# Two index-query units in one opening, the bias table in another visit, one weight load held back

## The chip, the cores and the metric

The kernel runs on 1 core of a Trainium2 chip. Its time is the device time of one execution in microseconds (us). Three runs of the kernel before gave 461.08, 461.11 and 461.12 us, the median is 461.11 us. TensorE is called PE here, VectorE DVE, ScalarE ACT, GpSimd POOL, and SyncE, which only issues transfers, SP.

## What is computed

One layer with two token mixers side by side: a gated linear recurrence (HGRN2), and a sparse attention in which a small indexer picks the keys. The input is 512 tokens of 1024 channels; one wide projection feeds everything. What the change touches is the indexer (projections `qi`, `ki`, `wi`) and the relative-position bias of the attention.

```python
proj = jnp.einsum('bld,dn->bln', x, w_in) + b_in
qa, fa, ia, za, qb, kb, vb, zb, qi, ki, wi, ga, gb = jnp.split(proj, cuts, axis=-1)
...
dots = jnp.einsum('bthd,bsd->bths', qi, kif) * (IDX_DIM ** -0.5)
score = jnp.einsum('bth,bths->bts', wb * (IDX_HEADS ** -0.5), jax.nn.relu(dots))
score = jnp.where(causal[None], score, -jnp.inf)
_, idx = lax.top_k(score, topk)
...
logits = jnp.einsum('bthd,btkhd->bhtk', qh, ks) * (HEAD_DIM_B ** -0.5)
bias = rel_bias[t5_bucket(qpos[None, :, None] - idx)]
p = jax.nn.softmax(logits + bias, axis=-1)
...
merged = jax.nn.sigmoid(ga) * ua + jax.nn.sigmoid(gb) * ub
return layer_norm(ALPHA * x + jnp.einsum('bld,de->ble', merged, w_out), ln_g, ln_b)
```

## The kernel before

The order of all work is written out by hand: each engine has a program of its own, and semaphores tie them together. The projection is cut into 31 units of 256 output columns (`UNITS`; unit 0 is `kiwi`, the index keys and index weights, with 72 columns), and four units of the output projection follow. Each engine's program walks over quarters q of a unit: unit u has the quarters 4u to 4u+3, of 12 matmuls each. What an engine does beside the units at a quarter stands in its `side(q)`. Such an insertion into PE's row of unit matmuls is called a visit here: the index dots (`dots`, from quarter 12 on), the scores and their transposes, the tree of the recurrence (`tree`).

Every product is made in three matmuls, as both operands are split into a rounded high part and a low part: hi x hi, hi x lo, lo x hi (`split_product`, L511 to L513). The contraction of 1024 runs over eight tiles k of 128. So a unit needs, per tile, a piece of the weights (512 KB per half of a unit, transfer on SP's queue into `w_raw`, which has two places, u % 2), ACT's rounding to `w_hi` (L825), and the subtraction that gives `w_lo`. POOL does that subtraction for most units (L1637), DVE for units 0 and 1 and for late ones (L1458). The input's tiles are treated alike: `x_in` (L467), `x_hi` by ACT (L843), `x_lo` by DVE (L1166).

The opening is special, since the input itself is only arriving. `opening()` on PE has 72 matmuls: 24 for `kiwi` into bank 6 and 48 for unit 1 (`qi0`, its halves i = 0 and 1 in banks 0 and 1). For k = 0 to 3 it goes kiwi, half 0, half 1; then kiwi and half 0 for k = 4 to 7, and last half 1 for k = 4 to 7. Unit 2 (`qi1`) is an ordinary unit behind it. Ahead of the opening stand WARM = 10 matmuls on a tile of ones (L784), which compute nothing that is used.

Results leave the banks in `leave_bank(u, i)` on ACT and DVE; PE may use a projection bank again when `proj_out[i]` has counted up. `turn_wi` (PE, at quarter 8) transposes the index weights by four matmuls of 8 columns (L593), DVE scales them (`scale_w`). `t5_table` (PE, after quarter 9) makes the bias table by one matmul of float32 with 384 columns (L779; it shows as two records); DVE copies it, SP writes it to HBM and reads it back in slanted rows. The first dots come at quarter 12.

SP issues its transfers in program order and waits in that order: for unit u it waits until the low parts of unit u - 2 are done, since the place in `w_raw` is free then.

Of the kernel before, what the change touches and what calls it, by code (L numbers as in the profile page):

```python
# [92 lines left out]
FIRST_BEHIND = (0, 2, 4, 6)  # L93
WARM = 10
# [13 lines left out]
def hybrid_kernel(nc, x_t, x_tok, w_units, w_kiwi, b_cols, b_ia, b_vb, lb_cols, g_cols, rel_bias,  # L108
                  ln_g, ln_b, one_hot, ident, causal, tree_masks, out):
    with ExitStack() as ctx:  # L110
# [116 lines left out]
        kiwi_bank = out_bank[0]  # L227
        up_bank = log_bank + turn_bank
# [6 lines left out]
        first_in = [sem(f"first_in{j}") for j in range(KT // 2)]  # L235
# [217 lines left out]
        def _(sp):  # L453
# [12 lines left out]
            for k in range(KT):  # L466
                sp.dma_start(x_tile(k), x_t[:, k, :]).then_inc(x_in[k], 16)  # L467
                if k in FIRST_BEHIND:
                    j = FIRST_BEHIND.index(k)
                    c = slice(2 * j * UW, 2 * j * UW + 2 * UW)  # L470
                    sp.dma_start(w_raw[:, 1, c], w_units[0][:, c]).then_inc(first_in[j], 16)
                if k == 1:
                    sp.dma_start(flat(kiwi_raw[:, KT // 2:KT, :]), w_kiwi[:, KT // 2 * WKI:]).then_inc(kiwi_in[1], 16)
            sp.dma_start(bias[:], b_cols).then_inc(early_in, 16)
            sp.dma_start(id_sb[:], ident).then_inc(early_in, 16)
            for u in range(2, NU):
                if u >= 3:
# [31 lines left out]
        def _(pe):  # L509
# [27 lines left out]
            def opening():  # L537

                def kiwi(k):
                    dst, first, last = kiwi_bank[0:WKI, :], k == 0, k == KT - 1  # L540
                    pe.wait_ge(kiwi_hi_done, k // 4 + 1)
                    pe.wait_ge(x_hi_done, k + 1)
                    nc.tensor.matmul(dst, kiwi_hi[:, k, :], x_hi[:, k, :], start=first, stop=False)
# [1234 lines left out]
```

## Time and profile before

| what | value |
|---|---|
| median of 3 runs | 461.11 us (461.08 to 461.12) |
| profiled execution, its own time | 461.16 us |
| its span, first to last instruction | 459.4 us |
| PE busy | 450.5 us, 98% of the span |
| DVE / ACT / POOL busy | 292.7 / 223.1 / 163.0 us |
| read from HBM | 43.04 MB |
| mean granted clock of PE | 0.996 |

The 461.16 us are the time of the execution whose trace is read; 1.76 us of it lie outside the span. Matmul records overlap: each lasts 0.39 us, but the next begins 0.23 us after it, and so the distance of starts is what one costs. A row of a timeline gives the start, the duration, the engine with the line of the code, what is written and read, and in brackets how long the engine was idle before and who ended that.

### The profile page before, as it was taken

How to read it: one execution, taken by the hardware profiler on the slowest of the kernel's cores; microseconds unless marked ns; L12 is line 12 of the kernel's file. 1: busy time of each engine (PE TensorE's matmuls, PEld its weight loads, DVE VectorE, ACT ScalarE, POOL GpSimd, SP SyncE). 2: the span in 40 equal slices, each digit the busy share in tenths (PEclk: the TensorE clock that was granted, in tenths of full speed). 3: DMA queues.
4: the chain of work that ended last, by engine and by line, in shares of the span. 5: the costliest groups of instructions: out<-in, count | busy, mean ns of one | idle time of the engine just before them, and what ended most of it. 6: DMA issues, size and time to landing. Idle time of an engine off the chain costs nothing.

```text
span 459.4 us, 7672 instructions
## 1 busy us (share of the span) xinstructions
PE 450.5 (98%) x2970; PEld 367.0 (80%) x2970; DVE 292.7 (64%) x557; ACT 223.1 (49%) x377; POOL 163.0 (35%) x161
## 2 busy tenths in 40 slices
PE   8999999999999999999999999999999999999993
PEld 6778888888888788888887887787788888888882
DVE  4445589999999853346989985871543241662286
ACT  5645445253345746294877474834774314341000
POOL 0444432583159813581004000000064454984000
PEclk9999999999999999999999999999999999999998
DMA  8808122256023720205020222022034222374022
GB/s 270 283 23 282 65 91 93 91 145 223 0 93 83 194 92 1 93 1 159 25 94 1 95 93 93 1 96 91 0 117 159 92 92 93 113 253 183 0 91 93
DMA packets 17156, 47.74 MB, mean 104 GB/s; under 512 B 2488, under 2 KB 4064, under 8 KB 17120
## 3 DMA queue, kind: packets, MB, share of 16 engines
q1 hardware_dynamic: 16880, 47.05, 31.3%
q8 instruction: 24, 0.39, 0.3%
q10 hardware_dynamic: 240, 0.20, 0.1%
q14 instruction: 12, 0.10, 0.1%
HBM read 43.04 MB, written 2.11 MB: 98 GB/s over the span
## 4 chain that ended last, share of the span: by engine, by line
PE 96%; DVE 1%; DMA 1%; ACT 1%; issue 0%; DVEq 0%; SPq 0%; ACTq 0%
PE bank L511 27%; PE bank L512 26%; PE bank L513 26%; PE bank L668 2%; PE bank L653 2%; PE bank L715 2%; PE bank L740 2%; PE bank L644 1%; PE bank L643 1%; DMA w_raw<-in_w_units 1%; PE bank L633 1%; PE bank L632 1%; PE bank L557 1%; PE bank L553 1%; PE bank L554 1%; PE bank L726 1%
## 5 line engine op out<-in xcount | busy, mean ns | idle before, releaser
L1637 POOL TENSOR_TENSOR w_lo<-w_raw,w_hi 128x512 fp32r<-128x512 f32 x92 | 122.0, 1354 | 162.3 <-ACT w_hi L825 162.3
L511 PE MATMUL bank<-x_hi,w_hi 128*128 128x512 f32 x336 | 133.4, 397 | 0.0
L512 PE MATMUL bank<-x_lo,w_hi 128*128 128x512 f32 x336 | 131.1, 390 | 0.0
L513 PE MATMUL bank<-x_hi,w_lo 128*128 128x512 f32 x336 | 131.0, 390 | 0.0
L511 PEld LDWEIGHTS bank<-x_hi,w_hi 128*128 128x128 f32 x336 | 63.1, 188 | 13.9 <-issue 0.8
L513 PEld LDWEIGHTS bank<-x_hi,w_lo 128*128 128x128 f32 x336 | 63.1, 188 | 13.7
L512 PEld LDWEIGHTS bank<-x_lo,w_hi 128*128 128x128 f32 x336 | 63.1, 188 | 12.0
L825 ACT ACTIVATE w_hi<-w_raw 128x1024 fp32r<-128x1024 f32 (+1 forms) x66 | 66.3, 1026 | 10.6 <-PE bank L513 5.5
L914 ACT ACTIVATE prob<-prob,nmax 128x128 f32<-128x128 f32 (+3 forms) x32 | 17.7, 554 | 41.6 <-DVE nmax L1289 41.5
L1265 DVE MAX8 best<-score 128x8 f32<-128x256 f32 (+2 forms) x48 | 26.8, 559 | 1.1
L1277 DVE COPY prob_t<-bank 128x128 f32<-128x128 f32 (+3 forms) x32 | 14.2, 485 | 19.0 <-PE bank L653 18.9
L1266 DVE MATCH_REPLACE8 score<-best,score 128x256 f32<-128x256 f32 (+2 forms) x48 | 26.0, 542 | 0.0
L511 PE MATMUL bank<-w_hi,x_hi 128*128 128x512 f32 x64 | 25.3, 395 | 0.0
L513 PE MATMUL bank<-w_hi,x_lo 128*128 128x512 f32 x64 | 25.0, 390 | 0.0
L512 PE MATMUL bank<-w_lo,x_hi 128*128 128x512 f32 x64 | 24.9, 390 | 0.0
L511 PE MATMUL bank<-o_hi,w_hi 128*128 128x512 f32 x64 | 24.9, 389 | 0.0
L512 PE MATMUL bank<-o_lo,w_hi 128*128 128x512 f32 x64 | 24.9, 389 | 0.0
L513 PE MATMUL bank<-o_hi,w_lo 128*128 128x512 f32 x64 | 24.9, 389 | 0.0
L1458 DVE TENSOR_TENSOR w_lo<-w_raw,w_hi 128x512 fp32r<-128x512 f32 x36 | 23.2, 683 | 1.3 <-ACT w_hi L825 1.2
L904 ACT ACTIVATE relus<-bank 128x256 f32<-128x256 f32 (+2 forms) x24 | 10.5, 490 | 21.4 <-PE bank L633 21.4
L1255 DVE SCALAR_TENSOR_TENSOR score<-relus,w_idx,score 128x256 f32<-128x256 f32 (+2 forms) x21 | 15.7, 749 | 7.9 <-ACT relus L904 6.2
L1655 POOL TENSOR_TENSOR logit<-t,pen 128x256 f32<-128x256 f32 x24 | 17.5, 744 | 9.1 <-DVE nmax L1289 9.1
(205 smaller groups left out, 753.1 us busy)
## 6 DMA issues: line engine op xcount, KB each, us to landing
w_raw<-in_w_units SPq DMA_DIRECT2D x66, 512.0 KB, 4.7
out<-y_sb SPq DMA_DIRECT2D x8, 256.0 KB, 2.0
x_raw_hi<-in_x_t SPq DMA_DIRECT2D x4, 256.0 KB, 5.7
w_raw<-in_w_units SPq DMA_DIRECT2D x4, 256.0 KB, 6.0
x_raw_lo<-in_x_t SPq DMA_DIRECT2D x4, 256.0 KB, 6.2
t_turned<-t_row SPq DMA_DIRECT2D x1, 1024.0 KB, 9.7
q_hi_g<-q_hi_g SPq DMA_DIRECT2D x8, 128.0 KB, 3.9
x_res_hi<-in_x_tok SPq DMA_DIRECT2D x2, 512.0 KB, 5.0
```

Source lines behind the costliest of these rows:

```text
L511: nc.tensor.matmul(dst, a_hi, b_hi, start=first, stop=False)
L512: nc.tensor.matmul(dst, a_hi, b_lo, start=False, stop=False)
L513: return nc.tensor.matmul(dst, a_lo, b_hi, start=False, stop=last)
L825: nc.scalar.activation(split_target(u, kiwi_hi, x_hi, w_hi)[:, k, :], raw(u)[:, k, :], ACT.Copy).then_inc(done, 1)
L914: nc.scalar.activation(prob[:, i % 4, 0:n], prob[:, i % 4, 0:n], ACT.Exp, bias=nmax[:, i % 4:i % 4 + 1], scale=-1.0, accum_out=prob_sum[:, ...
L1255: ins = nc.vector.scalar_tensor_tensor(out=score[b][:], in0=relus[:, i % 2, 0:n], scalar=w, in1=score[b][:], op0=ALU.mult, op1=ALU.add)
L1265: link(nc.vector.max(best8[:], score[b][:]))
L1266: link(nc.vector.match_replace(score[b][:], best8[:], score[b][:], TAKEN))
L1277: nc.vector.tensor_copy(prob_t[:, i % 4, 0:n], turn_bank[i % 2][:, 0:n]).then_inc(turn_out[i % 2], 1)
L1458: nc.vector.tensor_tensor(split_target(u, kiwi_lo, x_lo, w_lo)[:, k, :], raw(u)[:, k, :], split_target(u, kiwi_hi, x_hi, w_hi)[:, k, :].bi ...
L1637: nc.gpsimd.tensor_tensor(split_target(u, kiwi_lo, x_lo, w_lo)[:, k, :], raw(u)[:, k, :], split_target(u, kiwi_hi, x_hi, w_hi)[:, k, :].bi ...
L1655: nc.gpsimd.tensor_tensor(logit[:, i % 2, n - band:n], t5[:, h, 2 * P - band:], pen[b][:, n - band:] if b else causal_sb[:], ALU.add).then ...
```

## The change

Four things are done.

1. The opening takes in unit 2 and has 120 matmuls. For k = 0 to 5 PE runs the halves of unit 1 (banks 0 and 1) and of unit 2 (banks 7 and 5); then k = 6 and 7 of unit 1, all of `kiwi`, and k = 6 and 7 of unit 2. The weights of unit 2 are loaded, rounded and subtracted in four pieces, beside those of unit 1; unit 1's come in five pieces, the first two of one tile each. POOL makes unit 2's low parts as before. Both transfers of `kiwi` are issued behind x, on SP; one of them was ACT's first instruction. DVE treats `kiwi` last.
2. There are 8 matmuls ahead of the opening in place of 10.
3. `turn_wi` moves from quarter 8 to quarter 12 and carries the table's matmul, in other columns of the same bank; `t5_table` goes. Unit 4 is loaded before SP waits for the table, and the table's way to HBM follows unit 4.
4. SP loads unit 21 only when the tree's level 4 of the first head pair has been multiplied (quarter 77).

```diff
-FIRST_BEHIND = (0, 2, 4, 6)
-WARM = 10
+FIRST = ((0, 1), (1, 2), (2, 4), (4, 6), (6, 8))
+WARM = 8
...
+        first_bank = proj_bank, (out_bank[1], turn_bank[1])
...
             for k in range(KT):
                 sp.dma_start(x_tile(k), x_t[:, k, :]).then_inc(x_in[k], 16)
-                if k in FIRST_BEHIND:
+                for j in first_piece(k):
...
                     sp.dma_start(w_raw[:, 1, c], w_units[0][:, c]).then_inc(first_in[j], 16)
-                if k == 1:
-                    sp.dma_start(flat(kiwi_raw[:, KT // 2:KT, :]), w_kiwi[:, KT // 2 * WKI:]).then_inc(kiwi_in[1], 16)
+                if k % 2 == 0:
+                    c = slice(k * UW, k * UW + 2 * UW)
+                    sp.dma_start(w_raw[:, 0, c], w_units[1][:, c]).then_inc(second_in[k // 2], 16)
+            for a in range(2):
+                k = slice(a * KT // 2, (a + 1) * KT // 2)
+                sp.dma_start(flat(kiwi_raw[:, k, :]), w_kiwi[:, k.start * WKI:k.stop * WKI]).then_inc(kiwi_in[a], 16)
...
-            for u in range(2, NU):
-                if u >= 3:
-                    wait_lo(sp, u - 2, 4)
+            for u in range(3, NU):
+                wait_lo(sp, u - 2, 4)
+                if u == 21:
+                    wait_lvl_multiplied(sp, 0, 4)
...
+                if u == 4:
                     sp.wait_ge(table_done, 1)
                     sp.dma_start(t5_row, table[:]).then_inc(row_out, 16)
...
+                def queries_product(u, i, k):
+                    c, dst = slice(i * P, i * P + P), first_bank[u - 1][i][:]
+                    if (u, i) == (1, 0):
+                        pe.wait_ge(x_hi_done, k + 1)
+                        for j in first_piece(k):
+                            pe.wait_ge(first_hi_done, j + 1)
+                    elif i == 0:
+                        wait_hi(pe, 2, k // 2)
+                    nc.tensor.matmul(dst, w_hi[:, slot(u), k, c], x_hi[:, k, :], start=(k == 0), stop=False)
+                    if (u, i) == (1, 0):
+                        pe.wait_ge(x_lo_done, k + 1)
+                    nc.tensor.matmul(dst, w_hi[:, slot(u), k, c], x_lo[:, k, :], start=False, stop=False)
+                    if (u, i) == (1, 0):
+                        for j in first_piece(k):
+                            pe.wait_ge(first_lo_done, j + 1)
+                    elif i == 0:
+                        wait_piece(2, k)
+                    mm = nc.tensor.matmul(dst, w_lo[:, slot(u), k, c], x_hi[:, k, :], start=False, stop=(k == KT - 1))
...
+                tiles = [(1, 0), (1, 1), (2, 0), (2, 1)]
+                for k in range(KT - 2):
+                    for u, i in tiles:
+                        queries_product(u, i, k)
+                for u, i in tiles[:2]:
+                    for k in range(KT - 2, KT):
+                        queries_product(u, i, k)
+                for k in range(KT):
                     done = kiwi(k)
                 done.then_inc(part_done, 1)
+                for u, i in tiles[2:]:
+                    for k in range(KT - 2, KT):
+                        queries_product(u, i, k)
...
-                mm.then_inc(wi_turned, 1)
+                pe.wait_ge(table_in, 32)
+                nc.tensor.matmul(turn_bank[0][0:HEADS_B, P:P + T5W], rel_sb[:], hot_sb[:], start=True,
+                                 stop=True).then_inc(wi_turned, 1)
...
-            act.dma_start(flat(kiwi_raw[:, 0:KT // 2, :]), w_kiwi[:, 0:KT // 2 * WKI]).then_inc(kiwi_in[0], 16)
             for k in range(KT):
                 round_x(k)
-                if k in FIRST_BEHIND:
-                    split_first(FIRST_BEHIND.index(k))
-            split_hi(2, 0)
-            split_hi(2, 1)
+                for j in first_piece(k):
+                    split_first(j)
+                if k % 2 == 0:
+                    split_second(k // 2)
```

The start of PE's program before, behind the branch: `kiwi` works into bank 6, the halves of unit 1 into banks 0 and 1.

```order
L784 MATMUL bank5<-ones_sb 128x128 x10
L543 MATMUL bank6<-x_hi,kiwi_hi 72x512
L545 MATMUL bank6<-x_hi,kiwi_lo 72x512
L547 MATMUL bank6<-x_lo,kiwi_hi 72x512
L553 MATMUL bank0<-x_hi,w_hi 128x512
L554 MATMUL bank0<-x_lo,w_hi 128x512
L557 MATMUL bank0<-x_hi,w_lo 128x512
L553 MATMUL bank1<-x_hi,w_hi 128x512
L554 MATMUL bank1<-x_lo,w_hi 128x512
L557 MATMUL bank1<-x_hi,w_lo 128x512
```

The same place now: banks 7 and 5 are the halves of unit 2.

```order
L799 MATMUL bank5<-ones_sb 128x128 x8
L559 MATMUL bank0<-x_hi,w_hi 128x512
L562 MATMUL bank0<-x_lo,w_hi 128x512
L568 MATMUL bank0<-x_hi,w_lo 128x512
L559 MATMUL bank1<-x_hi,w_hi 128x512
L562 MATMUL bank1<-x_lo,w_hi 128x512
L568 MATMUL bank1<-x_hi,w_lo 128x512
L559 MATMUL bank7<-x_hi,w_hi 128x512
L562 MATMUL bank7<-x_lo,w_hi 128x512
L568 MATMUL bank7<-x_hi,w_lo 128x512
```

Ahead of the ninth of these matmuls there is now a wait for POOL's first low part of unit 2, and the three of `kiwi` stand no longer at the head.

SP's program at its start before, with x_raw the input and w_raw unit 1 (128x512 is 256 KB, 128x288 is 144 KB):

```order
L467 DMA x_raw_hi<-in_x_t 128x512
L471 DMA w_raw<-in_w_units 128x512
L467 DMA x_raw_hi<-in_x_t 128x512
L473 DMA kiwi_raw<-in_w_kiwi 128x288
L467 DMA x_raw_hi<-in_x_t 128x512
L471 DMA w_raw<-in_w_units 128x512
```

And now, where L478 loads unit 1 (128x256 is 128 KB) and L481 unit 2:

```order
L475 DMA x_raw_hi<-in_x_t 128x512
L478 DMA w_raw<-in_w_units 128x256
L481 DMA w_raw<-in_w_units 128x512
L475 DMA x_raw_hi<-in_x_t 128x512
L478 DMA w_raw<-in_w_units 128x256
L475 DMA x_raw_hi<-in_x_t 128x512
L478 DMA w_raw<-in_w_units 128x512
L481 DMA w_raw<-in_w_units 128x512
```

Unit 2's first piece has become the third transfer of the queue; it was behind x and unit 1.

The visits of PE from quarter 8 to 12 before (bank 4 takes the transposed index weights and the table, banks 2 and 3 the first dots):

```order
L593 MATMUL bank4<-id_sb,score3 128x8 x4
L511 MATMUL bank0<-x_hi,w_hi 128x512
...
L779 MATMUL bank4<-hot_sb,rel_sb 8x384
L511 MATMUL bank1<-x_hi,w_hi 128x512
...
L632 MATMUL bank2<-k_hi2,q_hl 128x256
L633 MATMUL bank2<-k_lo2,q_hl 128x256
```

And now, at quarter 12:

```order
L526 MATMUL bank0<-x_hi,w_lo 128x512
L613 MATMUL bank4<-id_sb,score3 128x8 x4
L616 MATMUL bank4<-hot_sb,rel_sb 8x384
L654 MATMUL bank2<-k_hi2,q_hl 128x256
L655 MATMUL bank2<-k_lo2,q_hl 128x256
```

Three visits have become one.

## Rows read from the trace of the kernel before

**Rows 1.** The page: busy us by engine, and two of the lines in 40 slices.
```profile
PE 450.5 (98%) x2970; PEld 367.0 (80%) x2970; DVE 292.7 (64%) x557; ACT 223.1 (49%) x377; POOL 163.0 (35%) x161
PEclk9999999999999999999999999999999999999998
```
**Rows 2.** Timeline of PE, opening: start us, us, what.
```profile
1.06 4.23 PE L784 MATMUL bank<-ones_sb 128*128 128x128 f32 x20 [1.06 <-POOL eps L1628]
5.04 0.47 PE L543 MATMUL bank<-x_hi,kiwi_hi 128*72 128x512 f32 x1
5.35 0.40 PE L545 MATMUL bank<-x_hi,kiwi_lo 128*72 128x512 f32 x1
5.59 0.39 PE L547 MATMUL bank<-x_lo,kiwi_hi 128*72 128x512 f32 x1
6.69 0.50 PE L553 MATMUL bank<-x_hi,w_hi 128*128 128x512 f32 x1 [0.70 <-ACT w_hi L825]
...
8.45 0.39 PE L543 MATMUL bank<-x_hi,kiwi_hi 128*72 128x512 f32 x1
...
22.85 0.41 PE L511 MATMUL bank<-x_hi,w_hi 128*128 128x512 f32 x1
```
**Rows 3.** Chain that ended last, first 9 us: start us, us, what.
```profile
1.18 4.80 DMA w_raw<-in_w_units
```
**Rows 4.** Timeline of ACT, opening.
```profile
4.03 0.63 ACT L843 ACTIVATE x_hi<-x_raw_hi 128x512 fp32r<-128x512 f32 x1 [2.01 <-DMA x_raw_hi<-in_x_t]
6.01 0.63 ACT L825 ACTIVATE w_hi<-w_raw 128x512 fp32r<-128x512 f32 x1 [1.34 <-DMA w_raw<-in_w_units]
7.40 0.63 ACT L843 ACTIVATE x_hi<-x_raw_hi 128x512 fp32r<-128x512 f32 x1 [0.77 <-DMA x_raw_hi<-in_x_t]
```
**Rows 5.** Timeline of DVE, opening.
```profile
4.23 0.31 DVE L1466 CAST kiwi_hi<-kiwi_raw 128x288 fp32r<-128x288 f32 x1 [4.23 <-DMA kiwi_raw<-in_w_kiwi]
4.80 0.68 DVE L1166 TENSOR_TENSOR x_lo<-x_raw_hi,x_hi 128x512 fp32r<-128x512 f32 x1
```
**Rows 6.** Timeline of POOL, its first low parts.
```profile
17.06 5.04 POOL L1637 TENSOR_TENSOR w_lo<-w_raw,w_hi 128x512 fp32r<-128x512 f32 x4 [16.06 <-ACT w_hi L825]
```
**Rows 7.** Timeline of PE, the three visits.
```profile
25.39 0.39 PE L513 MATMUL bank<-x_hi,w_lo 128*128 128x512 f32 x1
25.70 0.41 PE L593 MATMUL bank<-id_sb,score 8*128 8x8 f32 x4
26.04 0.50 PE L511 MATMUL bank<-x_hi,w_hi 128*128 128x512 f32 x1
...
28.69 0.39 PE L513 MATMUL bank<-x_hi,w_lo 128*128 128x512 f32 x1
29.01 0.81 PE L779 MATMUL bank<-hot_sb,rel_sb 32*8 32x384 f32 x2
29.75 0.50 PE L511 MATMUL bank<-x_hi,w_hi 128*128 128x512 f32 x1
...
37.81 0.39 PE L513 MATMUL bank<-x_hi,w_lo 128*128 128x512 f32 x1
...
38.57 0.40 PE L511 MATMUL bank<-x_hi,w_hi 128*128 128x512 f32 x1
```
**Rows 8.** Timeline of ACT, last half of unit 2 leaves its bank.
```profile
35.52 1.40 ACT L863 ACTIVATE q_hl<-bank,bias 64x512 fp32r<-64x512 f32 x2 [5.01 <-PE bank L513]
```
**Rows 9.** Timeline of DVE, the same half.
```profile
36.24 1.52 DVE L1203 SCALAR_TENSOR_TENSOR q_hl<-bank,bias,q_hl 64x512 fp32r<-64x512 f32 x2 [4.31 <-ACT q_hl L863]
```
**Rows 10.** Timeline of SP, weights of the units 21 to 23.
```profile
253.69 24.81 SPq L456 DMA_DIRECT2D w_raw<-in_w_units  x6
```
**Rows 11.** Timeline of PE, the visit of levels 3 and 4.
```profile
258.08 1.32 PE L715 MATMUL bank<-q_c,k_c 128*32 128x16 f32 x128
```
**Rows 12.** Timeline of ACT, first half of unit 21 is rounded.
```profile
265.73 1.05 ACT L825 ACTIVATE w_hi<-w_raw 128x1024 fp32r<-128x1024 f32 x1
```
**Rows 13.** Tile w_raw from 240 to 330 us: its transfers from issue to landing.
```profile
DMA to landing us min/median/max: 3.8/4.7/5.7
```

More of the change, by code:

```diff
@@ L234, in hybrid_kernel @@
         w_in = [[sem(f"w_in{j}_{a}") for a in range(2)] for j in range(2)]
-        first_in = [sem(f"first_in{j}") for j in range(KT // 2)]
+        first_in = [sem(f"first_in{j}") for j in range(len(FIRST))]
+        second_in, second_hi_done = [sem(f"second_in{j}") for j in range(KT // 2)], sem("second_hi_done")
         early_in = sem("early_in")
@@ L539, in kiwi @@
                 def kiwi(k):
[L540 to L543, printed above, removed]
+                    if k % 4 == 0:
+                        pe.wait_ge(kiwi_hi_done, k // 4 + 1)
                     wait_piece(0, k)
-                    nc.tensor.matmul(dst, kiwi_lo[:, k, :], x_hi[:, k, :], start=False, stop=False)
@@ L546, in kiwi @@
-                    pe.wait_ge(x_lo_done, k + 1)
-                    return nc.tensor.matmul(dst, kiwi_hi[:, k, :], x_lo[:, k, :], start=False, stop=last)
-                def first_qi(i, k):
-                    c, dst = slice(i * P, i * P + P), proj_bank[i][:]
-                    if i == 0:
-                        wait_hi(pe, 1, k // 2)
-                    nc.tensor.matmul(dst, w_hi[:, 1, k, c], x_hi[:, k, :], start=(k == 0), stop=False)
-                    nc.tensor.matmul(dst, w_hi[:, 1, k, c], x_lo[:, k, :], start=False, stop=False)
-                    if i == 0:
-                        wait_piece(1, k)
-                    return nc.tensor.matmul(dst, w_lo[:, 1, k, c], x_hi[:, k, :], start=False, stop=(k == KT - 1))
@@ L754, in side @@
             def side(q):
[L756 removed]
+                if q == Q_DOTS:
                     turn_wi()
@@ L862, in leave_bank @@
                     for h in (2 * tile, 2 * tile + 1):
-                        nc.scalar.activation(q_hl[rows(h), h, :], proj_bank[i][rows(h), :], ACT.Identity,
+                        nc.scalar.activation(q_hl[rows(h), h, :], first_bank[u - 1][i][rows(h), :], ACT.Identity,
                                              bias=bias[rows(h), c:c + 1]).then_inc(q_hi_done, 1)
@@ L1203, in leave_bank @@
                         ins = nc.vector.scalar_tensor_tensor(
-                            out=q_hl[rows(h + 1), h, :], in0=proj_bank[i][rows(h), :], scalar=bias[rows(h), c:c + 1],
+                            out=q_hl[rows(h + 1), h, :], in0=first_bank[u - 1][i][rows(h), :], scalar=bias[rows(h), c:c + 1],
                             in1=q_hl[rows(h), h, :].bitcast(F32), op0=ALU.add, op1=ALU.subtract)
@@ L1451, in gate_branch_a, with split_first @@
                                                op0=ALU.mult, op1=ALU.mult).then_inc(branch_a, 1)
+            def split_first(j):
+                dve.wait_ge(first_hi_done, j + 1)
+                k = slice(*FIRST[j])
+                nc.vector.tensor_tensor(w_lo[:, 1, k, :], raw(1)[:, k, :], w_hi[:, 1, k, :].bitcast(F32),
+                                        ALU.subtract).then_inc(first_lo_done, 1)
             def split_lo(u, j):
@@ L1580, in side @@
                     merge(m)
+            for k in range(KT):
+                split_x(k)
+                for j in first_piece(k):
+                    split_first(j)
             for j in range(KT // 2):
```

74 lines of the change are left out of this document (30 added, 44 removed).

## The prediction

> **What bounds the kernel now.** I read the busy line of the page first: PE is busy for 450.5 us of the 459.4 us span, DVE for 292.7, ACT for 223.1 [rows 1]. So a change is worth what it takes out of PE's row, or puts into it. The matmuls that do the work are all still there: 72 of the old opening and 48 of unit 2 are the 120 of the new one. What can change is the start, a hole, or the price of a visit. I then read PE's timeline of the first 23 us [rows 2]. The warm-up is over at 5.04 us, three matmuls of `kiwi` follow, and then PE stands 0.70 us until 6.69, waiting for ACT's `w_hi`. From 8.45 to 22.85 us it has no hole: 63 matmuls in 14.40 us, 0.2286 us each. Counted back from 22.85 by 72 x 0.2286 = 16.46, the opening before is as good as one that starts at 6.39 us and never stops. I call this its ideal start, and the new opening is measured the same way. Last I read the three visits between 25 and 39 us, and the load of unit 21.
>
> What sets 6.39 is a transfer: unit 1's first 256 KB was issued at 1.18 and took 4.80 us, to 5.98 [rows 3]; ACT rounds it from 6.01 for 0.63 us [rows 4].
>
> **The opening.** The first matmul now needs x tile 0 and 128 KB of unit 1. By 4.23 us, x tile 0 (256 KB) and the first half of `kiwi` (144 KB) had landed, for ACT and DVE start on them at 4.03 and 4.23 [rows 4, 5]. These 400 KB are about the 384 KB now wanted, so I let the weights land between 4.3 and 5.0. ACT is free at 4.66 and rounds 256 columns in some 0.4 us, an estimate below its 0.63 for 512. First matmul: 5.1 to 5.4. It needs no better, as six matmuls (1.4 us) lie before unit 2 is wanted.
>
> The seventh and eighth matmul need unit 2's `w_hi`, the ninth its `w_lo`, and that comes from POOL. The chain is landing, ACT, POOL, PE:
> - The landing. Issued third on SP's queue, after 256 + 128 KB. Up to its end 640 KB have to come in. Before, 656 KB (x, unit 1, `kiwi`'s first half) were in at 5.98 [rows 3]. By place in the queue, the third transfer of SP before was x tile 1, on which ACT started at 7.40 [rows 4], then with 768 KB on that queue; by bytes of that queue alone, 640 lies halfway between 512 (5.98) and 768 (7.40), at 6.69. The other end: if the 144 KB that left ACT's queue are pure gain, they give back their share of unit 1's 4.80 us, 144 / 656 x 4.80 = 1.05, and it is 4.95. I take 6.1, near the row with almost the same bytes.
> - ACT: 0.03 + 0.63 [rows 3, 4]. To 6.76.
> - POOL: four pieces took 5.04 us, 1.26 each [rows 6]; I take 1.30 for one alone. A handover between engines is 0.05 us, as from ACT's end at 6.64 to PE's start at 6.69 [rows 2, 4]. To 8.11.
> - The ninth matmul starts at 8.16. Eight are before it, so the ideal start is 8.16 - 8 x 0.2286 = 6.33, that is the landing + 0.23. Against 6.39 that is **-0.06 us**, with the ends -1.2 (landing 4.95) and +0.5 (landing 6.69).
>
> Behind k = 0 nothing is late. Each k now lasts 12 x 0.2286 = 2.74 us on PE and asks ACT for an x tile (0.63) and one tile each of two units (together 0.63), DVE for an x tile (0.68) and half a weight piece (0.34), POOL for half a piece (0.65). x tile 1 landed at 7.40 and its low part takes until 8.8, needed at 6.33 + 12 x 0.2286 + 0.23 = 9.3. The bytes per k rise from 420 KB in 2.06 us to 512 KB in 2.74 us, which is less per us.
>
> **Warm-up.** Twenty records of 128 columns stand between 1.06 and 5.04, 0.199 us each, or 1.55 ns a column [rows 2]; the table's two records of 384 columns take 0.74 us, at most 0.96 ns a column [rows 7]. So the warm-up runs at the lower of PE's two levels, 1.2 GHz, though the granted clock reads 9 tenths or more from the first slice [rows 1]. The level rises about where the first matmuls of `kiwi` stand: starts 5.04, 5.35, 5.59, that is 0.31 and then 0.24. Eight matmuls end at about 1.06 + 8 x 0.398 = 4.24, and PE then stands for up to 1.1 us. If the rise comes as before, this costs nothing. If the first eight matmuls of the opening run at the lower level, they take 8 x 0.427 = 3.4 us (512 columns at 1.2 GHz) and end at 8.7 rather than 8.16: +0.5, and the wait for POOL hides the rest. I take 0.
>
> The Trainium skill (TensorE: Matmul & The Clock Gate, Part 1) says that the throttled state is the default and that activity releases it. The trace agrees, with the 0.199 us per record. By that rule, two warm-ups fewer and a longer pause speak against this edit; the +0.5 above is what it would make of the sum.
>
> **The visits.** Each is priced as the distance of the starts around it, less 0.23 for the matmul in front, and with 0.11 where the matmul behind lasts 0.50 in place of 0.39 [rows 7]. `turn_wi`: 26.04 - 25.39 - 0.23 + 0.11 = 0.53. Table: 29.75 - 28.69 - 0.23 + 0.11 = 0.94. First dots: 38.57 - 37.81 - 0.23 = 0.53. Together 2.00 us. Merged there is one way in (25.70 - 25.62 = 0.08), the transposes (26.04 - 25.70 = 0.34), the table (0.74), the dots (0.53), and once the 0.11: 1.80 at most, and 1.69 if the way out vanishes into the dots. Below that, 0.34 for four tiny transposes is mostly draining, which the table may hide: down to 1.5. I take 1.70: **-0.30 us**, ends 0 and -0.5.
>
> The merged visit could wait for what is queued before it on ACT and DVE, since the dots need all of `qi1`. Unit 2 now ends at 6.33 + 120 x 0.2286 = 33.8. Before, ACT began its last half at 35.52, as soon as PE had it, and DVE ended at 37.76, 2.24 after that start [rows 8, 9]. Now ACT has more ahead: `kiwi` ends 12 matmuls earlier, at 31.1, its two moves begin some 0.2 us later and take about the 1.40 of these two, then comes the second half of unit 3 (1.05, as for any 1024 columns [rows 12]), then the first half of `qi1` (1.40), so the last begins at 35.15 and DVE ends at 37.4. The dots are due at 33.8 + 12 x 0.2286 + 1.16 = 37.7. The table's matmul covers what it needs; the margin is 0.3 us. I take 0, with an end at +0.3.
>
> Behind the waiting DVE stand the first scores, whose `relus` ACT makes, and PE's dots two further on; a visit comes every 3.2 us (12 matmuls and some 0.5), so a short copy of the table between them is hidden. The table itself is copied after quarter 13's scores, at about 37.7 + 3.2 + 2 = 43 us. SP waits for it with unit 5's load behind it, which has 4.7 us to landing [rows 13] and which ACT wants at quarter 16, about 37.7 + 4 x 3.2 = 50; PE wants unit 5 at quarter 20, near 60. Should ACT stand there for 1 us, the next dots have 2 us of slack. Nothing.
>
> **Unit 21.** Its load was issued at 253.69 [rows 10]. Now it follows level 4's matmuls, which end near 259.4 [rows 11]. With 3.8 to 5.7 us to landing [rows 13], the first half is in at 263.2 to 265.1, and ACT takes it at 265.73 [rows 12]. PE has no hole there that a quieter memory could close, so it gives nothing and costs nothing: 0, with +-0.1 as ends.
>
> **Sum.** -0.06 - 0.30 = -0.36 us against the profiled execution's 461.16 (its span of 459.4 and 1.76 outside), which is 0.05 above the median of 461.11. Forecast: **460.8**, with its own range 460.2 to 461.3. About 0.2%, 0.9 us, is what I count as told from no change; the bounds are 460.2 and 462.0.
>
> **Rivals.**
> - *The transfers come early.* Without `kiwi` beside it unit 2 lands at 4.95 and the ideal start is 5.18: -1.2, with the visits -1.5, **459.7**. For it: the 144 KB really are gone from the first 4 us. Against it: x tile 0, with almost nothing before it, still took until 4.03, so start-up time weighs more than bytes. The Trainium skill (DMA: Bandwidth & Descriptors, Issuing engines are not separate DMA queues) says that transfers of all issuing engines run on the same 16 engines and interleave. By that rule the removal from ACT's queue does help SP's. Chance 0.20.
> - *POOL's low part is the new wait, and it is late.* Unit 2's first piece lands at its place in the queue, 7.40, as the third transfer before; then the ideal start is 7.63: +1.24, less 0.30 of visits, +0.94, **462.1**, slower. It decides from a landing of 6.46 on (there it eats the visits' gain). For it: the longest chain of engines in the opening now feeds the ninth matmul. Against it: the bytes ahead are fewer. Chance 0.12.
> - *The merged visit saves nothing*, as `qi1` is not ready by 0.3 us: **461.1**. For it: a margin of 0.3 us only. Chance 0.13.
> - *The clock rises late* by the shorter warm-up: +0.5 to +1.5, according to how many matmuls beyond the eighth stay at 0.427. With the visits 461.3 to 462.3, **461.6**. Chance 0.07.
>
> The forecast keeps 0.48. Faster by over 0.2%: most of the first rival and a little of the forecast, 0.20. Slower: half of the second and a fifth of the clock's, 0.07. The same: 0.73. The range 459.7 to 461.8 leaves out most of the second rival's cases and the far ends of the first and the last.
>
> **What would show it.** Right: PE's ninth opening matmul starts near 8.2 us with an idle time before its weight load that POOL's `w_lo` ends; the last opening matmul of unit 2 near 33.6; one visit of 1.7 us at about 36.5; dots straight behind the table; no new PE wait near 265 us. Wrong: unit 2's first `w_hi` outside 5.6 to 6.6; starts 0.43 apart beyond the eighth matmul; a wait of the dots for DVE's `q_hl`; or anything over 0.3 us after 60 us.

## The result and the profile after

The changed kernel takes 461.92 us (median of 20 runs, 461.45 to 462.74); the kernel before, run beside it, 461.28 us (20 runs, 460.96 to 461.56). The ratio is 1.0014, its 95% interval 1.0008 to 1.002: slower by 0.64 us, where 0.36 faster was forecast. The profiled execution of the changed kernel took 461.93 us, its span is 460.1, the mean granted clock 0.995.

The page, which answers to [rows 1]: busy us by engine, and the granted clock in 40 slices.
```profile
PE 450.2 (98%) x2966; PEld 366.7 (80%) x2966; DVE 295.5 (64%) x558; ACT 223.7 (49%) x380; POOL 163.6 (36%) x161
PEclk9999999999999999999999999999999999999997
```
PE has less to do (450.2 after 450.5) in a longer span (460.1 after 459.4). So the loss is idle time of PE, and I read the waits of PE next: what it waited for, us in total, times, the longest.
```profile
PE bank L799 <- POOL eps L1652: 1.1, 1, 1.1
PE bank L654 <- DVE q_hl L1219: 0.9, 1, 0.9
PE bank L568 <- POOL w_lo L1661: 0.6, 1, 0.6
PE bank L559 <- ACT w_hi L837: 0.3, 1, 0.3
```
The first stands ahead of the warm-up in either kernel. The third was forecast. The second is the wait of the first dots that the prediction named as a sign against it. The timeline of PE shows both places; its first rows answer to [rows 2], the last to [rows 7].
```profile
4.78 0.47 PE L559 MATMUL bank<-x_hi,w_hi 128*128 128x512 f32 x1
...
6.95 0.50 PE L559 MATMUL bank<-x_hi,w_hi 128*128 128x512 f32 x1 [0.31 <-ACT w_hi L837]
...
8.31 0.50 PE L568 MATMUL bank<-x_hi,w_lo 128*128 128x512 f32 x1 [0.63 <-POOL w_lo L1661]
...
33.96 0.39 PE L524 MATMUL bank<-x_hi,w_hi 128*128 128x512 f32 x1
...
36.45 0.39 PE L526 MATMUL bank<-x_hi,w_lo 128*128 128x512 f32 x1
36.77 0.41 PE L613 MATMUL bank<-id_sb,score 8*128 8x8 f32 x4
37.11 0.81 PE L616 MATMUL bank<-hot_sb,rel_sb 32*8 32x384 f32 x2
38.77 0.35 PE L654 MATMUL bank<-k_hi,q_hl 128*128 128x256 f32 x1 [0.85 <-DVE q_hl L1219]
...
39.32 0.40 PE L524 MATMUL bank<-x_hi,w_hi 128*128 128x512 f32 x1
...
61.92 0.39 PE L526 MATMUL bank<-x_hi,w_lo 128*128 128x512 f32 x1
```
From PE's timeline of the kernel before, the first matmul of unit 3 and the last unit matmul before the visit near 61 us:
```profile
35.32 0.39 PE L511 MATMUL bank<-x_hi,w_hi 128*128 128x512 f32 x1
...
61.17 0.39 PE L513 MATMUL bank<-x_hi,w_lo 128*128 128x512 f32 x1
```
These rows give the account of the profiled executions:
- The opening. Unit 3 began at 35.32, with two visits of 0.53 and 0.94 before it; without them at 33.85. Now it begins at 33.96: **+0.11 us**.
- The merged visit. It costs 39.32 - 36.45 - 0.23 = 2.64 us, of which 0.85 are the wait. Without it 1.79, where three visits were 2.00: **-0.21 us**.
- The wait for `q_hl`: **+0.85 us**. (The split is by the records. In e2 below, where nothing waits, the same visit costs 1.74; by it the wait costs 0.90 and the merging gives 0.26, with the same sum.)

That is +0.75, and 61.92 - 61.17 is 0.75 too. The distance stays at 0.74 to 0.76 us at every later visit up to 326 us, so nothing behind 40 us counts: not unit 21, not the later table. The profiled executions differ by 0.77.

Why `q_hl` is late stands in the timeline of DVE. The first group is of the kernel after, the second of the kernel before; the last row answers to [rows 9].
```profile
32.91 0.74 DVE L1209 SCALAR_TENSOR_TENSOR k_lo<-bank,bias,k_hi 64x512 fp32r<-64x512 f32 x1 [4.50 <-ACT score L875]
33.69 0.42 DVE L1213 CAST k_lo<-k_lo 64x512 fp32r<-64x512 f32 x1
34.03 1.51 DVE L1214 CAST k_hi<-k_hi 64x512 fp32r<-64x512 f32 x1
35.47 3.05 DVE L1219 SCALAR_TENSOR_TENSOR q_hl<-bank,bias,q_hl 64x512 fp32r<-64x512 f32 x4
```
```profile
24.08 0.42 DVE L1197 CAST k_lo<-k_lo 64x512 fp32r<-64x512 f32 x1
24.42 0.41 DVE L1198 CAST k_hi<-k_hi 64x512 fp32r<-64x512 f32 x1
24.75 1.51 DVE L1203 SCALAR_TENSOR_TENSOR q_hl<-bank,bias,q_hl 64x512 fp32r<-64x512 f32 x2
```
The copy of the keys' high part to the other 64 partitions (SBUF to SBUF) takes 1.51 us in place of 0.41. What began just before it is in the timeline of POOL, kernel after; its first rows answer to [rows 6].
```profile
6.97 1.28 POOL L1661 TENSOR_TENSOR w_lo<-w_raw,w_hi 128x512 fp32r<-128x512 f32 x1 [5.96 <-ACT w_hi L837]
10.75 1.29 POOL L1661 TENSOR_TENSOR w_lo<-w_raw,w_hi 128x512 fp32r<-128x512 f32 x1 [2.50 <-ACT w_hi L837]
...
33.97 2.73 POOL L1661 TENSOR_TENSOR w_lo<-w_raw,w_hi 128x512 fp32r<-128x512 f32 x2 [2.90 <-ACT w_hi L837]
```
POOL begins the third low part of unit 3 at 33.97, DVE the copy at 34.03, and the copy ends at 35.54, a little after POOL's first piece: POOL's next piece begins at 35.22, and takes 1.48 us, 0.2 longer than the 1.27 of a piece alone, while the copy is still ending. ACT is at work beside the copy too, on the high parts of the queries:
```profile
33.92 2.82 ACT L880 ACTIVATE q_hl<-bank,bias 64x512 fp32r<-64x512 f32 x4
```
In the kernel before POOL began unit 3 only at 25.78, 1.36 us after the copy's start:
```profile
25.78 5.02 POOL L1637 TENSOR_TENSOR w_lo<-w_raw,w_hi 128x512 fp32r<-128x512 f32 x4 [3.68 <-ACT w_hi L825]
```
Theory P: DVE is held by POOL's instruction, `q_hl` ends at 38.52 rather than about 37.4, and PE stands. Rivals: the clock, by the shorter warm-up (C); the queues of ACT and DVE are too long even without POOL (Q); or the merged visit itself costs more than it saves (M).

### The profile page after: what moved, and what is told of

The parts are those of the page before. It is cut to its first block, busy times and chain, and to the rows that moved or that the text cites. A ratio compares the mean times of both kernels' runs of the same rounds, so it can differ in the third digit from the quotient of the medians.

```text
span 460.1 us, 7668 instructions
## 1 busy us (share of the span) xinstructions
PE 450.2 (98%) x2966; PEld 366.7 (80%) x2966; DVE 295.5 (64%) x558; ACT 223.7 (49%) x380; POOL 163.6 (36%) x161
## 4 chain that ended last, share of the span: by engine, by line
PE 94%; DVE 2%; DMA 1%; ACT 1%; issue 0%; POOL 0%; SPq 0%; DVEq 0%; ACTq 0%
PE bank L524 26%; PE bank L525 25%; PE bank L526 25%; PE bank L675 2%; PE bank L690 2%; PE bank L737 2%; PE bank L762 2%; PE bank L568 1%; PE bank L562 1%; PE bank L559 1%; PE bank L666 1%; PE bank L665 1%; DMA w_raw<-in_w_units 1%; PE bank L654 1%; PE bank L655 1%; PE bank L748 1%
## 5 line engine op out<-in xcount | busy, mean ns | idle before, releaser
L524 PE MATMUL bank<-x_hi,w_hi 128*128 128x512 f32 x320 | 126.9, 397 | 0.0
L525 PE MATMUL bank<-x_lo,w_hi 128*128 128x512 f32 x320 | 124.9, 390 | 0.0
L526 PE MATMUL bank<-x_hi,w_lo 128*128 128x512 f32 x320 | 124.7, 390 | 0.0
L837 ACT ACTIVATE w_hi<-w_raw 128x1024 fp32r<-128x1024 f32 (+2 forms) x69 | 67.1, 991 | 9.9 <-PE bank L526 5.5
L526 PEld LDWEIGHTS bank<-x_hi,w_lo 128*128 128x128 f32 x320 | 60.1, 188 | 13.0
L524 PEld LDWEIGHTS bank<-x_hi,w_hi 128*128 128x128 f32 x320 | 60.1, 188 | 12.5 <-ACT q_a L913 0.3
L525 PEld LDWEIGHTS bank<-x_lo,w_hi 128*128 128x128 f32 x320 | 60.1, 188 | 11.5
L1481 DVE TENSOR_TENSOR w_lo<-w_raw,w_hi 128x512 fp32r<-128x512 f32 x32 | 20.4, 682 | 0.0
L1271 DVE SCALAR_TENSOR_TENSOR score<-relus,w_idx,score 128x256 f32<-128x256 f32 (+2 forms) x21 | 14.3, 682 | 8.7 <-ACT relus L921 7.0
```

The source lines that it names most:

```text
L524: nc.tensor.matmul(dst, a_hi, b_hi, start=first, stop=False)
L525: nc.tensor.matmul(dst, a_hi, b_lo, start=False, stop=False)
L526: return nc.tensor.matmul(dst, a_lo, b_hi, start=False, stop=last)
L837: nc.scalar.activation(split_target(u, kiwi_hi, x_hi, w_hi)[:, k, :], raw(u)[:, k, :], ACT.Copy).then_inc(done, 1)
L1271: ins = nc.vector.scalar_tensor_tensor(out=score[b][:], in0=relus[:, i % 2, 0:n], scalar=w, in1=score[b][:], op0=ALU.mult, op1=ALU.add)
L1481: nc.vector.tensor_tensor(split_target(u, kiwi_lo, x_lo, w_lo)[:, k, :], raw(u)[:, k, :], split_target(u, kiwi_hi, x_hi, w_hi)[:, k, :].bi ...
```

## The experiments

| run | what | median us (n) | ratio to before, 95% |
|---|---|---|---|
| e1 | after, POOL waits for the copy | 461.26 (11) | 0.9994, 0.9986 to 1.0003 |
| e10 | the same again | 461.27 (11) | 1.0001, 0.9992 to 1.0009 |
| e2 | after, ACT rounds first | 461.20 (11) | 0.9994, 0.9986 to 1.0003 |
| e9 | after, again | 462.04 (11) | 1.0016, 1.0007 to 1.0025 |
| e12 | before, with the overlap made | 461.32 (10) | 1.0, 0.9991 to 1.0009 |
| e5 | e2, table apart | 461.93 (11) | 1.0009, 1.0 to 1.0018 |
| e3 | before, 8 warm-ups | 461.86 (11) | 1.0015, 1.0005 to 1.0025 |
| e11 | the same again | 461.40 (11) | 1.0005, 0.9996 to 1.0014 |
| e7 | after, 10 warm-ups | 462.54 (8) | 1.0025, 1.0014 to 1.0035 |
| e4 | before, unit 21 held back | 461.23 (11) | 1.0, 0.9991 to 1.0009 |
| e6 | e2, DVE makes unit 2's first low part | 460.51 (11) | 0.9985, 0.9976 to 0.9993 |
| e8 | e6, 10 warm-ups | 460.44 (11) | 0.9981, 0.9973 to 0.999 |

The kernel before stood at 461.35 beside e1 to e4, at 461.27 beside e5 to e8, and at 461.29 beside e9 to e12. The ratio isn't the quotient of these medians, so the two can differ: for e1 the medians are 0.09 us apart, the ratio says 0.28. A difference below some 0.4 us, the half width of these intervals, isn't told from nothing.

### The overlap taken away: e1 and e10

```diff
                 # POOL, the low parts of a unit, piece by piece
+                if u == 3 and j == 2:
+                    pool.wait_ge(k_twice, 2)
```


> The changed kernel, but POOL waits with the third low part of unit 3 until DVE has copied the keys to the other partitions (k_twice). Nothing else moves. Theory P (DVE's copy of the keys, 1.51 us where it took 0.41 before, is held up by POOL's subtraction that runs at the same time, and this is what makes q_hl late and PE wait 0.85 us at the first dots): the copy takes 0.41 again, DVE ends q_hl near 37.6 instead of 38.5, PE's wait of 0.85 us falls to under 0.1, the time falls by 0.8 us against the changed kernel, to some 0.15 us below the kernel before. Theory Q (ACT and DVE simply have too much queued behind kiwi, POOL is beside the point): the copy stays at 1.5 us or DVE ends no earlier than 38.3, PE's wait stays above 0.6, the time is that of the changed kernel, +0.6 us against the kernel before.

Timeline of DVE, e1:
```profile
34.27 0.41 DVE L1214 CAST k_hi<-k_hi 64x512 fp32r<-64x512 f32 x1
34.88 3.06 DVE L1219 SCALAR_TENSOR_TENSOR q_hl<-bank,bias,q_hl 64x512 fp32r<-64x512 f32 x4 [0.19 <-ACT q_hl L880]
```
Timeline of POOL and of PE, e1:
```profile
34.77 2.54 POOL L1663 TENSOR_TENSOR w_lo<-w_raw,w_hi 128x512 fp32r<-128x512 f32 x2 [3.46 <-DVE k_hi L1214]
```
```profile
36.70 0.39 PE L526 MATMUL bank<-x_hi,w_lo 128*128 128x512 f32 x1
...
37.35 0.81 PE L616 MATMUL bank<-hot_sb,rel_sb 32*8 32x384 f32 x2
38.20 0.35 PE L654 MATMUL bank<-k_hi,q_hl 128*128 128x256 f32 x1
...
38.74 0.40 PE L524 MATMUL bank<-x_hi,w_hi 128*128 128x512 f32 x1
```
The copy is back at 0.41, and the view has no wait of the dots any more. Some 0.1 us of it is left: the dots begin 0.85 us behind the table's start, in e2 0.73, and 0.26 behind the end of `q_hl` (37.94), the same distance as in the kernel after (0.25). The copy is the same instruction on the same data as in the kernel after; of what bears on it, only POOL's start moved. ACT is no rival: it works on `q_hl` from 34.16 for 2.82 us here, beside a copy (34.27) of 0.41. To exclude a difference between chips, e10 repeats e1 on one chip with e9, the changed kernel again.

> The first experiment once more (POOL waits with unit 3's third low part for the copies of the keys), beside the changed kernel. Theory P: 0.6 to 0.85 us below the changed kernel. Theory Q: as the changed kernel.

> The changed kernel as it is, beside the next one on the same chip, so that the two are compared directly. Theory P: 461.9, +0.6 us against the kernel before, PE waits 0.85 us for DVE's q_hl, the copy of the keys lasts 1.5 us. If the wait were an accident of one profiled execution, it would be missing here.

In e9 the wait of 0.85 and the copy of 1.51 are there again, in e10 neither, and e10 is 0.77 us below e9 (461.27 and 462.04). The merged visit costs 39.15 - 36.29 - 0.23 = 2.63 us in e9 and 39.18 - 37.13 - 0.23 = 1.82 in e10. The two profiled executions themselves both took 461.75: in that of e10 unit 3 began 0.84 us later (34.63 and 33.79), since unit 2's `w_hi` began at 6.92 and not at 6.08. One wait of POOL, added in two lines, takes back what the change lost. P stands, and Q falls in its strong form, in which the first dots wait over 0.6 us without POOL.

### The overlap avoided by order: e2

```diff
                 # ACT, quarter 9
-                if q == 9:
-                    leave_bank(0, 0)
...
                 # the rounding of unit 3's second half stands here
+                if q == 9:
+                    leave_bank(0, 0)
```


> The changed kernel, but ACT rounds the second half of unit 3 before it takes kiwi out of its bank, instead of behind it. POOL's low parts of unit 3 then run from about 28.5 to 33.7 us, ahead of DVE's copies of the keys, and ACT has 1.06 us less between kiwi and q_hl. Theory P: the copies take 0.4 us each, q_hl is ready near 37.5, PE's wait of 0.85 is gone, time 0.8 us below the changed kernel (-0.15 to -0.25 against the kernel before). Theory Q: ACT's 1.06 us are what counts, q_hl is earlier by that too, so the time is the same as under P; but under Q the first experiment, in which ACT keeps its order, gains nothing. If neither holds, the wait stays at 0.85.

461.20 us: the same gain without the added wait. By itself e2 doesn't separate P from Q, since ACT's queue is shorter too; e1 does. POOL now works straight through from 28.85 for 5.05 us (four pieces), and the copy, at 34.35, lasts 0.41. The merged visit costs 38.75 - 36.78 - 0.23 = 1.74 us.

### The overlap made in the old kernel: e12

```diff
                 # ACT, old kernel: unit 3's first half is rounded ahead of qi0's last half
+                if q == 8:
+                    split_hi(3, 0)
...
-                    if q - hi_quarter(v) in (0, 1):
+                    if q - hi_quarter(v) in (0, 1) and (v, q) != (3, 8):
```


> The kernel before, in which ACT rounds unit 3's first half ahead of the last half of qi0, so that POOL's subtraction starts near 24.4 us, when DVE copies the keys. It makes the suspected collision in the kernel that did not have it. Theory P: the second key copy at 24.4 us lasts about 1.5 us in place of 0.41, ending about 0.3 us after POOL's first piece; DVE's q_hl, which read PSUM, keep 0.76 each; the time stays as before, as nothing waits there. Theory Q or chance: the copy stays at 0.41.

Timeline of DVE, then of POOL, e12:
```profile
24.50 1.51 DVE L1200 CAST k_hi<-k_hi 64x512 fp32r<-64x512 f32 x1
25.93 1.51 DVE L1205 SCALAR_TENSOR_TENSOR q_hl<-bank,bias,q_hl 64x512 fp32r<-64x512 f32 x2
```
```profile
24.44 3.97 POOL L1639 TENSOR_TENSOR w_lo<-w_raw,w_hi 128x512 fp32r<-128x512 f32 x3 [1.60 <-ACT w_hi L825]
```
Moving POOL's start to 0.06 us before the copy (24.44 and 24.50) lengthens it to the same 1.51 us in a kernel that has nothing else of the change. The time stays the same (461.32), since there PE waits for neither the copy nor what follows it. So the hold cost only where DVE's next result was awaited at once, as in the changed kernel.

### What the merging is worth: e5

```diff
                 # PE: the table's matmul between unit 1's last product and kiwi, alone
+                pe.wait_ge(table_in, 32)
+                nc.tensor.matmul(turn_bank[0][0:HEADS_B, P:P + T5W], rel_sb[:], hot_sb[:], ...)
...
                 # and no longer behind the four transposes
-                nc.tensor.matmul(turn_bank[0][0:HEADS_B, P:P + T5W], rel_sb[:], hot_sb[:], ...)
```


> The second experiment (ACT rounds unit 3 before it takes kiwi out), with the table's matmul taken out of the visit at quarter 12 and put alone between unit 1's last matmuls and kiwi. It prices the merging of the visits. Theory as in the prediction: a visit of its own pays its way in and out again (0.09 + 0.11), so PE spends 0.94 on the table there and 0.53 + 0.42 on the rest, the sum of the excess rises from 1.8 to about 2.0 us and the time by 0.2 us against the second experiment. Rival, the merging is worth nothing or more than 0.3 us: the same time, or +0.4.

Timeline of PE, e5:
```profile
25.29 0.39 PE L568 MATMUL bank<-x_hi,w_lo 128*128 128x512 f32 x1
25.60 0.81 PE L587 MATMUL bank<-hot_sb,rel_sb 32*8 32x384 f32 x2
26.34 0.45 PE L524 MATMUL bank<-x_hi,kiwi_hi 128*72 128x512 f32 x1
...
37.14 0.39 PE L526 MATMUL bank<-x_hi,w_lo 128*128 128x512 f32 x1
37.46 0.41 PE L616 MATMUL bank<-id_sb,score 8*128 8x8 f32 x4
38.39 0.36 PE L655 MATMUL bank<-k_hi,q_hl 128*128 128x256 f32 x1 [0.52 <-DVE q_hl L1220]
...
38.94 0.40 PE L524 MATMUL bank<-x_hi,w_hi 128*128 128x512 f32 x1
```
Alone the table costs 26.34 - 25.29 - 0.23 = 0.82, and 0.88 with the 0.06 by which the matmul behind it is longer; the other visit 38.94 - 37.14 - 0.23 = 1.57. Together 2.45, against 1.74 in e2: 0.71. The medians differ by 0.73, or by 0.81 if each is taken against the kernel before beside it (+0.66 and -0.15). The expectation had 0.2. The rest is a wait of 0.52 us: `q_hl` isn't ready when only four transposes stand ahead of the dots. So the merging itself saves 0.19, and the table's matmul covers another 0.52 of a wait that the earlier end of unit 2 brings in any case. Theory M falls, in the strong form that the merging costs something.

### The warm-up: e3, e11 and e7

```diff
-WARM = 10
+WARM = 8
```


> The kernel before, with 8 matmuls ahead of the opening instead of 10 and nothing else. Theory that the warm-up is without effect (as the prediction put it): within 0.2 us of the kernel before, the starts of kiwi's first matmuls at about 4.7, and 0.23 apart from the fourth on. Rival, the clock rises later with the shorter warm-up: starts 0.43 apart beyond 6.7 us and +0.3 to +1 us.

> The kernel before with 8 warm-up matmuls once more, since its +0.5 us stood in no row of its profile. If the shorter warm-up really costs: +0.3 to +0.7 us again, with runs beyond 462.3. If it was chance: within 0.2 us.

```diff
-WARM = 8
+WARM = 10
```


> The changed kernel with 10 matmuls ahead of the opening in place of 8. Theory C (with 8 the clock rises late in some executions, as the third experiment says, and this is part of the changed kernel's loss): the median falls by 0.2 to 0.5 us to 461.5 or so, and the slow tail over 462.2 goes. Rival, the wait for POOL at the ninth matmul hides a late clock in this opening: the same time as the changed kernel, 461.9, tail and all.

By their medians these don't settle: the same edit gave +0.51 us in e3 and +0.11 in e11 (each against before), the second within its interval of nothing, and in the changed kernel two more warm-ups gave 462.54 (e7), no gain. The spans say more, for each execution's span is on record beside its time.

- The middle span is 459.5 us in e3 and in e11, as in the kernel before beside them. In the two traces unit 3 begins at 35.31 and 35.39, after 35.32. So in the usual execution 8 warm-ups cost this kernel nothing within the span.
- e3's excess lies outside the span: in seven of its eleven executions 2.36 to 2.74 us are outside, where the 96 of the kernel before beside the experiments have 1.75 to 1.96. It doesn't follow the warm-up, for e7 with 10 warm-ups has seven of eight above 1.96 (up to 2.95), while of those with 8 e11 has one, e6 four, and e1, e2, e5, e9 and e10 none. What it is, no row says.
- Two executions of e3 and two of e11 have a span of 460.9 to 461.1, where none of those 96 is above 460.1. So 8 warm-ups seem to lose some 1.5 us now and then in the old opening. None of the four was profiled, and one of e7, with 10 warm-ups, has 461.7, as far above its middle; so neither how they lose it nor that the warm-up is the cause is shown.

e7's middle span, 460.15, is that of the changed kernel (460.1), and the wait of 0.85 is in its trace as well. So C doesn't explain the loss, and e10 lost all of it with 8 warm-ups in place.

### Unit 21: e4

```diff
                 # SP, old kernel, ahead of the load of unit 21
+                if u == 21:
+                    wait_lvl_multiplied(sp, 0, 4)
```


> The kernel before, with the load of unit 21 behind the tree's level 4 and nothing else. As the prediction put it: ACT rounds unit 21's first half at 265.7 as before, no new wait of PE, the same time within 0.1 us. Rival, the late load makes unit 21's rounding late or the quiet memory speeds up the chain of ACT and DVE near 256 us: more than 0.2 us either way, with the distance of PE's starts around 258 or 272 changed by as much.

461.23 us beside 461.35, nothing beyond the interval. Timeline of SP, which answers to [rows 10], and of ACT, which answers to [rows 12]:
```profile
259.52 18.94 SPq L456 DMA_DIRECT2D w_raw<-in_w_units  x6
```
```profile
265.69 1.05 ACT L827 ACTIVATE w_hi<-w_raw 128x1024 fp32r<-128x1024 f32 x1
```
The load is issued 5.8 us later, and ACT takes it at the same time.

### A version that beats both: e6 and e8

The remaining new wait is that of the ninth matmul for POOL. In e6, on top of e2, DVE makes that one low part, with a semaphore of its own; e8 also has 10 warm-ups.
```diff
                 # DVE, opening, k == 0
+                dve.wait_ge(second_hi_done, 1)
+                nc.vector.tensor_tensor(w_lo[:, slot(2), 0:2, :], raw(2)[:, 0:2, :],
+                                        w_hi[:, slot(2), 0:2, :].bitcast(F32),
+                                        ALU.subtract).then_inc(second_lo_done, 1)
...
                 # POOL
-                for piece in range(4):
+                for piece in range(u == 2, 4):
```


> The second experiment, with the first low part of unit 2 made by DVE in place of POOL. Theory P (POOL's 1.28 us stand in front of the ninth matmul, and hold up DVE's second x tile, 1.12 in place of 0.68): the ninth matmul starts 0.5 to 0.6 us earlier, near 8.0 in place of 8.6, the x tile takes 0.68, and the time falls by 0.5 us against the second experiment, to 460.7. Rival, the transfers or ACT are late behind it anyway: the gain at the ninth matmul is lost before k = 3, time as the second experiment.

> All three together: ACT rounds unit 3 first, DVE makes unit 2's first low part, 10 matmuls ahead of the opening. Theory P with C: below the kernel before by 0.7 to 1.0 us, some 460.5, and with a narrow spread. If the clock is no part of it, the same as the experiment with DVE alone. Rival, with 10 matmuls the opening starts later than its first weights and loses 0.1 us.

Timeline of DVE, e8, then of PE:
```profile
6.46 0.69 DVE L1616 TENSOR_TENSOR w_lo<-w_raw,w_hi 128x512 fp32r<-128x512 f32 x1 [0.96 <-ACT w_hi L840]
```
```profile
5.35 0.57 PE L562 MATMUL bank<-x_hi,w_hi 128*128 128x512 f32 x1
5.76 0.40 PE L565 MATMUL bank<-x_lo,w_hi 128*128 128x512 f32 x1
...
7.36 0.39 PE L571 MATMUL bank<-x_hi,w_lo 128*128 128x512 f32 x1
```
DVE needs 0.69 us for what took POOL 1.28, and DVE's second x tile is back at 0.69 us in both. The ninth matmul begins 1.57 us behind the start of `w_hi` (7.36 and 5.79), and 1.46 in e6 (7.87 and 6.41), where it was 2.05 in the kernel after (8.31 and 6.26); the rest of e8's early start is a landing 0.47 us earlier. The waits view of PE names nothing but the start of its warm-up. In e8 that warm-up is itself the bound: the first weights are rounded at 4.77, the first matmul begins at 5.35, and from 5.76 on they follow each other every 0.23 us past the ninth. e8 is 460.44 us: 0.83 below the kernel before, some 1.5 below the changed one. e6 without the longer warm-up is 460.51, the same within its spread, though its starts from the second to the sixth matmul stand 0.43 us apart; the expectation had 460.7. By the middle spans (458.5 and 458.6, before 459.5) the two are 1.0 and 0.9 below; four of e6's executions have 2.1 to 3.1 us outside the span.

## Why the prediction was wrong

The forecast was 460.8 us, the range 459.7 to 461.8; it came to 461.92 and slower.

**The step that failed** is the wait of the merged visit: "so the last begins at 35.15 and DVE ends at 37.4 ... the margin is 0.3 us. I take 0, with an end at +0.3." Only ACT's queue was recounted there. DVE's end was put 2.24 us behind ACT's last start, as in the kernel before, and neither DVE's own queue nor POOL was looked at. Before, POOL's work on unit 3 came behind the key copies; now the rounding of unit 3's second half lies just ahead of them, POOL starts at 33.97, and one copy takes 1.10 us more. DVE ended at 38.52, and the term was +0.85 where 0 to +0.3 was allowed.

The margin of 0.3 us wasn't there even without POOL. The dots begin 0.25 us behind the end of `q_hl` (38.77 and 38.52; 0.26 in e1 and e10), which the prediction left out, and without the hold DVE took 3.78 us for its part from ACT's start on the four (34.16 to 37.94 in e1), where the prediction had 1.40 + 2.24 = 3.64. From 0.3 that leaves 0.30 - 0.25 - 0.14 = -0.09, which is why e1 keeps some 0.1 us of the wait. The rival that the merged visit saves nothing had the right place, `qi1` not ready, but the wrong size: its cause was a margin missed by 0.3 us.

The same rows speak for a rule of the Trainium skill that I had not weighed (SBUF — State Buffer, Who interferes with whom): VectorE and GpSimd share one pair of SBUF ports, which is an exclusive lock. A VectorE copy or cast in a mode that uses both pairs waits for the whole GpSimd instruction if that was issued first, and an instruction with two inputs in SBUF contends with a GpSimd instruction that reads SBUF; one with at most one SBUF input, outside those modes, does not. The trace agrees on all three: the cast was 1.51 in place of 0.41, the subtraction of two SBUF tiles up to 1.78 in place of 0.68 (last section), and the SCALAR_TENSOR_TENSOR, of whose two tiles one comes from the bank in PSUM, took 0.76 each beside POOL's pieces (3.06 for four in e1, from 34.88, POOL at work from 34.77 to 37.31), as without POOL (1.51 for two). By this rule the copy had to be priced at the end of POOL's piece. With the 1.10 us that the rows show for it, DVE would have been put at 37.4 + 1.10 = 38.5, the wait at 0.8, and the sum at some +0.4 us, an estimate: slower.

**The opening**, -0.06 forecast, +0.11 measured. The mechanism was right: the chain landing, ACT, POOL sets the ninth matmul. Each link was somewhat later than its estimate: ACT at 6.26 for 6.13, POOL at 6.97 for 6.81, the matmul at 8.31 for 8.16. That is the landing. It is no constant: over seven profiled executions of this opening (after, e1, e2, e5, e7, e9, e10) the same rounding began between 6.08 (e9) and 6.92 (e10), and the ninth matmul between 8.12 and 8.96. The prediction's upper end for the landing, 6.69, was a little short. Unit 3's start, less e5's table visit of 0.88, lies -0.08 to +0.78 us from the 33.85 of before in these seven, the middle one at +0.35. So the +0.11 of the profiled execution is on the low side, and the term was mis-sized by more than that. The five traces with the old opening have the corresponding rounding between 5.85 and 6.09.

**The merged visit**, -0.30 forecast, -0.21 measured, and -0.26 in e2 (1.74). The term was mis-sized by 0.04 to 0.09 us.

**The warm-up**, 0 with an end at +0.5: right for the profiled execution. Its second and third matmul start 0.33 us behind the one before, but not for the clock: DVE ended `x_lo` at 5.05 and `w_lo` at 5.39, and they start at 5.11 and 5.45; the fifth and sixth stand 0.23 apart, the distance of the higher level. In e1 the distance is 0.42 to 0.43 up to 6.18, and the wait for `w_lo` covers it.

**Unit 21**, 0: right (e4). **Everything behind 40 us**, 0: right.

With the hold removed the change is worth -0.09 (e1) and -0.02 (e10) us, both within their intervals of nothing, where the sum without that step was -0.36. The profiled execution of e1 shows the sum at work: its unit 3 begins at 34.20, +0.35 after the 33.85 of before (`w_hi` at 6.47), its visit costs 38.74 - 36.70 - 0.23 = 1.81, that is -0.19, and it took 461.31 us, +0.15. So what the merging gives, a later landing takes. That the change without the hold comes out at nothing is shown; that it is the landing in all executions is read from the few profiled ones.

## What to carry to other kernels

When a change moves DVE's copies or its operations on two SBUF tiles, look at what POOL does in the same microsecond and price them at the end of POOL's instruction, not at their duration alone; here a margin below one POOL instruction (1.3 us) was no margin. Count the handover between the engines into it too (0.25 us here). Where a new wait stands at the head of the critical path, ask first which engine makes the awaited piece and whether a faster one is idle: here DVE instead of POOL for a single piece was worth more than all of the reordering (e6 stands 0.76 us below before, e2, which differs from it in this piece alone, 0.15). And a merged visit can be worth more by what its filler covers (0.52 us) than by what it saves (0.19).

## What the runs showed of the hardware

How long DVE is held by POOL's subtraction depends on which pieces overlap. Timeline of DVE, kernel after, in the opening (alone the first form takes 0.68, [rows 5]):
```profile
4.36 0.69 DVE L1182 TENSOR_TENSOR x_lo<-x_raw_hi,x_hi 128x512 fp32r<-128x512 f32 x1 [4.36 <-ACT x_hi L860]
7.68 1.12 DVE L1182 TENSOR_TENSOR x_lo<-x_raw_hi,x_hi 128x512 fp32r<-128x512 f32 x1 [2.29 <-ACT x_hi L860]
11.34 1.25 DVE L1182 TENSOR_TENSOR x_lo<-x_raw_hi,x_hi 128x512 fp32r<-128x512 f32 x1 [0.63 <-ACT x_hi L860]
...
13.94 1.56 DVE L1182 TENSOR_TENSOR x_lo<-x_raw_lo,x_hi 128x512 fp32r<-128x512 f32 x1
16.03 1.78 DVE L1473 TENSOR_TENSOR w_lo<-w_raw,w_hi 128x512 fp32r<-128x512 f32 x1
```
The second and third end at 8.80 and 12.59, 0.55 us behind POOL's pieces (6.97 + 1.28 = 8.25 and 10.75 + 1.29 = 12.04), so nearly their own length after it; the fourth ends at 15.50, 0.55 behind the piece of 13.34 + 1.61, and the last at 17.81, 0.55 behind that of 15.92 + 1.34. The held copies of the keys end some 0.3 us behind POOL's piece, nearly their length too. It goes the other way round as well: POOL's piece of 13.34 took 1.61 us in place of 1.28, where DVE's subtraction of 13.12 (0.68 us) was already at work.

The clock's rise came at different matmuls in executions with the same warm-up. With 8 warm-ups, e6 has starts 0.43 us apart up to 7.10 us and e1 up to 6.18, while the kernel after has 0.23 from 5.78 on, and its first matmul (0.47 us long, 0.77 in e6) is already near the higher level. With 10, e7 has 0.42 up to 6.34 and e8 0.23 from 5.76. No row says why.

The time outside the span is not a constant either: 1.75 to 1.95 us in twelve of the fourteen profiled executions, 2.43 in e3 and 2.39 in e7, and up to 3.08 in an execution of e6 that was not profiled. Who compares kernels to a few tenths should look at the spans too.
